# Strassen's seven products for the q, k and recurrence-gate blocks of the second projection

## The chip, the cores and the metric

The kernel runs on one core of a Trainium2 chip. The metric is the device time of one execution in microseconds (us); lower is better. Three runs of the kernel before gave 1884.34, 1887.08 and 1887.52 us, median 1887.08 us.

## The reference, cut to what matters

Two transformer-like blocks follow each other on 2048 tokens of width 1024, all in 32-bit floats. The change lies in the input projection of the second block, which turns the normalised tokens `h` (2048 x 1024) into 36 groups of 128 columns and 16 gate columns:

```python
proj = h @ w_in + b_in
(na_q, na_k, na_v, na_z, ml_q, ml_k, ml_v, ml_o, ml_z,
 i_f, f_f, i_b, f_b) = jnp.split(proj, split_idx, axis=-1)
na_out = neighbourhood_attention(na_q, na_k, na_v, rpb) * jax.nn.silu(na_z)
qk = jax.nn.silu(centred_short_conv(jnp.concatenate([ml_q, ml_k], axis=-1), conv_w, conv_b))
# ... chunkwise recurrence forward and backward over ml_q, ml_k, ml_v and the gates ...
ml_out = hm * jax.nn.silu(ml_z)
return jnp.concatenate([na_out, ml_out], axis=-1) @ w_out
```

`na_q`, `na_k` and `ml_z` (512 columns each) are the blocks that the change computes in another way. `na_q` and `na_k` feed the attention, which begins right after the projection; `ml_z` is read in the last stage.

## The kernel before, in words

A 32-bit product is made from three TensorE matmuls: each operand is split into a high part (a rounding copy on ScalarE, `split_high`) and a low part (a subtraction on VectorE, `split_low`), and `mm3` (L145, L146, L147) issues high x high, high x low and low x high into one PSUM bank.

**The projection** (class `Proj`). The 36 groups of 128 columns are called units, four to a block; before, the order of the blocks is nq, nk, mv, mk, mq, gates, nv, nz, mz, mo (`BLOCKS`). A piece of work `n` is one unit times 512 tokens (for mv, nv and mo: 128 tokens times a whole block); it is 8 k-tiles times three matmuls, so 24 matmuls with 512 columns. There are 144 of these and 4 short ones for the gates. All engines run over the same list `work`, and each does its share of `n` in program order. Six units of split weights lie in SBUF (`wa`, `wb`), and all four token blocks (`hT`) lie there split. Weights for a unit come through two raw buffers (`iraw`, 512 KB each, issued by SyncE at L1389). A result leaves PSUM through ScalarE or VectorE (for nq and nk both, as high and low part; for mo VectorE adds the bias at L1653 and ScalarE takes the sigmoid at L1578), and GpSimd issues its store to HBM (L1676, L1678, L1694, L1697).

**The states** (class `States`) are cut into 31 steps `s` that ride along with the projection: `states.pe(n)` and so on are called behind the projection's part of `n` on every engine, from `s0` on. A step is: SyncE loads keys `skC` (L2312; once turned, in the second half, `kTD` at L2318) and values `sv` (L2322); GpSimd weighs the values (L2378); TensorE multiplies (L2397, eight matmuls) and, in the first 16 steps, transposes the next keys (L2409); ScalarE copies and stores the transposed keys; VectorE updates `state` (L2358) once the store of the last one has landed; SyncE stores it (`CD`, L2327). Keys for transposition of step `s` may be loaded only when step `s-1` is transposed, since there is one buffer. In TensorE's program the product of step `s-1` and the transposes of step `s` stand behind work `n = s0 + s`. Before, `s0` lies 21 pieces of work behind the start of nv, and the states run during nz, mz and part of mo. `Gates` are 17 small steps that come first.

**The attention** takes over at the end of mo. Its first loads (`early_sp`: q and k heads `hd` at L1835, then z, v and the tables) are issued at works 3, 7 and 11 of mo; its first scores (`first_pe`) stand before the last piece of mo; its first mask table is made on GpSimd (L2017, L2024).

Of the kernel before, what the change touches and what calls it, by code (L numbers as in the profile page):

```python
# [5 lines left out]
F32 = mybir.dt.float32  # L6
# [4 lines left out]
P = 128  # L11
# [1193 lines left out]
BLOCKS = [("nq", 0), ("nk", 1), ("mv", 6), ("mk", 5), ("mq", 4), ("nv", 2), ("nz", 3), ("mz", 8), ("mo", 7)]  # L1205
# [3 lines left out]
class Proj:  # L1209


    NU = 6
# [3 lines left out]
    def __init__(self, k, banks, out, gw):  # L1216
# [24 lines left out]
        self.conv_u, self.conv_out, self.row_step, self.sign = k.sem("conv_u"), k.sem("conv_out"), k.sem("row_step"), k.sem("sign")  # L1241
# [3 lines left out]
        self.cols = [b * W + j * P for _, b in BLOCKS for j in range(4)]  # L1245
        work = []
        for bi, (name, b) in enumerate(BLOCKS):
            u0 = 4 * bi
            if name == "nv":
                work += [("gates", 0, tb) for tb in range(TB)]  # L1250
            if name in ROW_BLOCKS:
                work += [(name, u0, m) for m in range(NT)]
            elif bi == 0:
                work += [(BLOCKS[u // 4][0], u, tb) for tb in range(TB) for u in range(NU)]
            else:
                units = range(u0 + 2, u0 + 4) if bi == 1 else range(u0, u0 + 4)
                work += [(name, u, tb) for u in units for tb in range(TB)]
# [5 lines left out]
        for n, (name, u, tb) in enumerate(work):  # L1263
            first = len(jobs)
            if n == 0:
                jobs += [("w", 2), ("w", 3)]
            elif n < 3:
                jobs.append(("w", n + 3))
            if 2 <= n < 6:
                jobs.append(("h", 1, n - 2))  # L1270
            if n == 3 * NU:
                jobs.append(("gates",))
            if NU <= n < 3 * NU and u < 4:
                jobs.append(("h", tb + 1, u))
# [5 lines left out]
            while nu < min(more, 36):  # L1280
# [15 lines left out]
        self.stage, nst, self.convs = {}, 0, {}  # L1296
        for n, (name, u, tb) in enumerate(work):
            if name in ("mq", "mk"):
                self.convs[n] = len(self.convs)
            else:  # L1300
                self.stage[n] = nst
                nst += 2 if name in ("nq", "nk") else 1
        self.users = {}
        for n, i in self.stage.items():
            self.users[i] = n
            if work[n][0] in ("nq", "nk"):
                self.users[i + 1] = n

        self.evac_at, self.row_at, self.sign_at, c = {}, {}, {}, 0
        for n, (name, u, tb) in enumerate(work):  # L1310
            c += {"nq": 4, "nk": 1, "nz": 1, "mz": 1, "gates": 1, "mo": 1}.get(name, 0)
# [3 lines left out]
            if name in ("nq", "nk", "mz"):  # L1315
# [1796 lines left out]
```

## Time and profile before

| | |
|---|---|
| median of 3 runs | 1887.08 us |
| span of the profiled execution | 1883.3 us |
| TensorE matmul busy | 1865.6 us, 99% |
| VectorE, ScalarE, GpSimd busy | 982.4, 618.3, 552.5 us |
| mean HBM traffic | 161 GB/s |
| projection with states | from 598 to 1442 us |

The profiled execution has no other time of its own than its span from the first to the last instruction; the 3.8 us between it and the median are what lies around it and the spread of the runs. Matmuls are pipelined: the 0.39 us that the page gives for one is its stay in the array, and a new one starts every 0.23 us.

### The profile page before, as it was taken

Reading aid. Unit: us, or ns where it says so; the run is one execution under the profiler, and the core shown is the slowest. Engines: PE = TensorE matmul, PEld = TensorE weight load, DVE = VectorE, ACT = ScalarE, POOL = GpSimd, SP = SyncE. Lnnn points to the kernel's source line nnn. Section 1 sums busy time; section 2 is a strip of 40 time slices with the busy share of each in tenths; the row PEclk is TensorE's granted clock in tenths of the full one; section 3 lists DMA queues with packets and bytes.
Section 4 is the critical chain, followed back from the end, with each engine's and each line's share of the span. In section 5 each row is a group of like instructions: output and inputs, shape, how many; then the busy total and the mean of one; then the engine's idle time right before and its main releaser. Section 6 shows DMA issues by size and latency. Waiting matters only on the chain.

```text
span 1883.3 us, 26698 instructions
## 1 busy us (share of the span) xinstructions
PE 1865.6 (99%) x10035; PEld 1540.4 (82%) x10035; DVE 982.4 (52%) x2117; ACT 618.3 (33%) x1317; POOL 552.5 (29%) x925
## 2 busy tenths in 40 slices
PE   9999999999999999999999999999999999999998
PEld 8888878888888888888888787888887777788886
DVE  6556565775666433114777322223213777776665
ACT  7321111233444432101222202221114667655552
POOL 2112222233642222110110000222314777544442
PEclk9999999999999999999999999999999999999999
DMA  6223142366897745312221123665563776867663
GB/s 197 95 79 119 62 128 81 104 184 235 306 266 252 235 168 162 101 50 84 74 78 68 53 62 116 211 211 171 168 220 105 243 232 224 271 219 241 230 229 112
DMA packets 236365, 303.55 MB, mean 161 GB/s; under 512 B 41414, under 2 KB 161126, under 8 KB 236204
## 3 DMA queue, kind: packets, MB, share of 16 engines
q1 hardware_dynamic: 205724, 215.84, 37.4%
q0 software_dynamic: 23600, 77.61, 11.4%
q10 hardware_dynamic: 6912, 8.39, 1.2%
q8 instruction: 80, 1.31, 0.3%
q14 instruction: 49, 0.40, 0.1%
HBM read 194.71 MB, written 107.54 MB: 160 GB/s over the span
## 4 chain that ended last, share of the span: by engine, by line
PE 94%; DVE 2%; DMA 2%; issue 1%; ACT 1%; POOL 0%; SPq 0%; POOLq 0%; DVEq 0%; ACTq 0%
PE banks L145 25%; PE banks L147 25%; PE banks L146 25%; PE banks L2106 3%; PE banks L2069 3%; PE banks L2088 3%; PE banks L2704 2%; PE banks L2706 1%; PE banks L2397 1%; DMA iraw<-in_w_in 1%; PE banks L2089 1%; PE banks L2674 1%; PE banks L234 1%; PE banks L1109 1%; PE banks L1741 0%
## 5 line engine op out<-in xcount | busy, mean ns | idle before, releaser
L145 PE MATMUL banks<-hT,wu 128*128 128x512 f32 (+1 forms) x528 | 204.6, 387 | 1.1 <-DVE wu L512 0.6
L147 PE MATMUL banks<-hT,wu 128*128 128x512 f32 (+1 forms) x528 | 202.3, 383 | 0.0
L146 PE MATMUL banks<-hT,wu 128*128 128x512 f32 (+1 forms) x528 | 202.2, 383 | 0.0
L145 PE MATMUL banks<-iT,wub 128*128 128x512 f32 x384 | 151.2, 394 | 0.0
L145 PE MATMUL banks<-iT,wua 128*128 128x512 f32 x384 | 150.8, 393 | 0.0
L145 PE MATMUL banks<-wub,iT 128*128 128x512 f32 x384 | 150.6, 392 | 0.0
L147 PE MATMUL banks<-iT,wub 128*128 128x512 f32 x384 | 149.7, 390 | 0.0
L147 PE MATMUL banks<-iT,wua 128*128 128x512 f32 x384 | 149.5, 389 | 0.0
L146 PE MATMUL banks<-wub,iT 128*128 128x512 f32 x384 | 149.5, 389 | 0.0
L147 PE MATMUL banks<-wub,iT 128*128 128x512 f32 x384 | 149.5, 389 | 0.0
L146 PE MATMUL banks<-iT,wua 128*128 128x512 f32 x384 | 149.5, 389 | 0.0
L146 PE MATMUL banks<-iT,wub 128*128 128x512 f32 x384 | 149.4, 389 | 0.0
L1653 DVE TENSOR_TENSOR st<-banks,br 128x512 f32<-128x512 f32 x48 | 33.1, 692 | 201.0 <-PE banks L147 193.5
L145 PEld LDWEIGHTS banks<-hT,wu 128*128 128x128 f32 x528 | 99.3, 188 | 25.3 <-ACT ub L470 4.3
L147 PEld LDWEIGHTS banks<-hT,wu 128*128 128x128 f32 x528 | 99.2, 188 | 19.6
L146 PEld LDWEIGHTS banks<-hT,wu 128*128 128x128 f32 x528 | 99.3, 188 | 18.5
L1932 ACT ACTIVATE p<-s,ast 128x480 f32<-128x480 f32 (+1 forms) x128 | 83.7, 655 | 53.0 <-DVE ast L1970 53.0
L145 PE MATMUL banks<-ws,ys 128*128 128x512 f32 x256 | 100.5, 393 | 0.0
L147 PE MATMUL banks<-ws,ys 128*128 128x512 f32 x256 | 99.8, 390 | 0.0
L146 PE MATMUL banks<-ws,ys 128*128 128x512 f32 x256 | 99.7, 389 | 0.0
L1618 DVE SCALAR_TENSOR_TENSOR ca<-cu,cw,ca 128x512 f32<-128x512 f32 (+2 forms) x128 | 96.3, 752 | 4.5
L2039 POOL TENSOR_SCALAR p<-p,ast 128x384 f32<-128x384 f32 (+1 forms) x128 | 71.9, 562 | 46.2 <-DVE ast L1976 44.8
(293 smaller groups left out, 4116.3 us busy)
## 6 DMA issues: line engine op xcount, KB each, us to landing
iraw<-in_w_in SPq DMA_DIRECT2D x36, 512.0 KB, 4.4
wa<-in_w_ada SPq DMA_DIRECT2D x48, 256.0 KB
yT<-sg POOLq DMA_DIRECT2D x32, 256.0 KB, 3.1
oraw<-yT SPq DMA_DIRECT2D x32, 256.0 KB, 4.8
xr<-in_x SPq DMA_DIRECT2D x16, 512.0 KB, 4.4
h<-h POOLq DMA_DIRECT2D x16, 512.0 KB, 4.3
hT<-tr POOLq DMA_DIRECT2D x16, 512.0 KB, 5.1
tws<-wg SPq DMA_DIRECT2D x16, 512.0 KB, 5.1
```

The costliest lines, as they stand in the source:

```text
L145: e.matmul(ps, lh, rh, start=first, stop=False)
L146: e.matmul(ps, lh, rl, start=False, stop=False)
L147: return e.matmul(ps, ll, rh, start=False, stop=last)
L234: t = e.transpose(self.tp[m][g][:, j * P:(j + 1) * P], self.x[m][:, (4 * g + j) * P:(4 * g + j + 1) * P], self.ident[:])
L1618: e.scalar_tensor_tensor(out=a[:, left:right], in0=cur[:, left + x:right + x], scalar=cw[:, x, ch:ch + 1], in1=a[:, left:right], op0=ALU.m ...
L1653: e.tensor_tensor(self.st[i % 2][:], pb, self.br[:, x % 2, :], ALU.add).then_inc(*self.row_step.inc())
L1932: e.activation(self.pr[n % 8][:, 0:N], self.sr[n % 4][:, 0:N], ACT.Exp, bias=self.st[:, n, 0:1], scale=-1.0, accum_out=self.st[:, n, 1:2]) ...
L2039: e.tensor_scalar(rows[:, :, 0:P], rows[:, :, 0:P], self.st[:, n, 2:3], 1.0, ALU.mult, ALU.mult).then_inc(*self.scaled.inc())
L2069: t = e.matmul(self.pS[(2 * p + hh) % 4][:, 0:N], b[r, q, (2 * i + a) * P:(2 * i + a + 1) * P], keys, start=x == 0, stop=x == 2)
L2088: e.transpose(self.pT[x][:, j * P:(j + 1) * P], probs[:, 160 * j:160 * j + P], self.ident[:])
L2106: t = e.matmul(self.pO[d, 0:P], v, self.ptr[(2 * q + hh) % 4][r, j * P:(j + 1) * P], start=(j == 0), stop=(j == nb))
L2704: t = e.matmul(o, self.eb[c % 2][d][:, h, :], self.v1[c % 2][:, h, :], start=True, stop=not self.inter(c, d))
```

## The change

The nq, nk and mz units leave `Proj` and go into a new class `Fast`, which runs between the projection and the attention. `Proj` keeps 24 units in the order nz, mk, mv, mq0, mq1, nv, mq2, mq3, gates, mo (`PLAN`) and starts with 5 units instead of 6. The states' steps start at the second work of mo (`g0`), so that 31 steps of the recurrence lie, but for their gates part, in `Fast`: one step behind every second product.

`Fast` works on six "doubles": three pairs of unit pairs (nq0,1 with nk0,1; nq2,3 with nk2,3; mz0,1 with mz2,3) for each half of the tokens (1024). A pair of units times two token blocks of 512 is a 2 x 2 block product, and so are the two halves of the inner dimension; Strassen's rule makes it from 7 products with half the inner length in place of 8. A product is 4 k-tiles times three matmuls, 12 matmuls with 512 columns. There are 84 (`N`), 14 in a double, and 48 outputs. Sums of token quarters (128 x 2048) and of weight quarters (128 x 512) are made on GpSimd, their high parts on ScalarE, their low parts on VectorE. Token sums stay for the three doubles of a half; weight sums are made for each product, in 8 slots. Products that belong to several outputs are added in PSUM, and partial sums go through `part` on VectorE.

```diff
+    N, ND, OUTS, SLOTS = 84, 6, 48, 8
+    SEQ = [(i, q) for i, q in ((5, 0), (5, 1), (2, 0), (2, 1), (1, 0), (3, 0), (1, 1), (3, 1), (4, 0), (4, 1), (6, 0), (6, 1), (7, 0), (7, 1))]
...
+        self.early_x = {7: (0, 5), 9: (0, 2), 11: (0, 1), 13: (0, 3), 15: (0, 4)}
+        self.late_x = {1: (0, 6), 5: (0, 7), 30: (1, 5), 37: (1, 2), 38: (1, 3), 40: (1, 1), 42: (1, 4), 45: (1, 6), 47: (1, 7)}
...
+        self.early_t = {15: (0, 1)}
...
+        for n in range(1, self.ND):
+            for p in range(14):
+                self.late_t[14 * n - 3 + 8 * p // 13].append(14 * n + p)
...
+    def slot_free(self, w, j):
+        if j >= self.SLOTS:
+            w.wait_ge(*self.full.ge(j - self.SLOTS + 1))
...
+    def unit_load(self, e, dst, n, q, sem):
+        name, j0 = self.DOUBLES[self.ORDER[n][1]][q]
+        for u in range(2):
+            c = COLUMNS[name] * W + (j0 + u) * P
+            e.dma_start(dst[u][:], self.proj.win[:, :, c:c + P]).then_inc(*sem.inc())
...
+    def early_act(self, e, w, m):
+        if m in self.early_x:
+            self.tokens_high(e, w, *self.early_x[m])
+        for j in self.early_t.get(m, ()):
+            self.weights_high(e, w, j)
...
+    def sp(self, e, att):
...
+        for j in range(self.N):
+            n, p = divmod(j, 14)
+            if p == 6 and n + 1 < self.ND:
+                w.wait_ge(*self.t_lo.ge(14 * n + 14))
+                self.unit_load(e, self.rx, n + 1, 0, self.rx_in)
+                if n:
+                    self.unit_load(e, self.ry, n + 1, 1, self.ry_in)
+            if j == 8:
+                for x in range(2):
+                    self.quarter_load(e, self.kept[x], 1, (0, x), self.kept_in)
+            for i, at in ((2, 32), (1, 35), (4, 38), (6, 40), (7, 42)):
+                if j == at:
+                    self.tokens_load(e, w, 1, i)
+            att.early_sp(e, w, j)
+            if j % 2 == 0:
+                self.states.sp(e, w, self.nw + j // 2)
...
+    def dve(self, e, att):
...
+            if i == 5:
+                w.wait_ge(*self.full.ge(j + 1))
...
+                e.tensor_copy(part[:], self.pp[q]).then_inc(*self.copied.inc())
...
+            for x in self.late_t[j]:
+                self.weights_low(e, w, x)
+            if j in self.late_x:
+                self.tokens_low(e, w, *self.late_x[j])
+            if j % 2 == 0:
+                self.states.dve(e, w, self.nw + j // 2)
...
+    def pe(self, e, att):
...
+            elif i == 1:
...
+                    w.wait_ge(*self.w_out.ge(4 * n + (3 if q else 0)))
...
+            w.wait_ge(*self.t_lo.ge(j + 1))
...
+            for c in range(KT // 2):
+                e.matmul(ps, t[:, 0, c], x[:, 0, c], start=new and c == 0, stop=False, skip_group_check=not new)
+                e.matmul(ps, t[:, 0, c], x[:, 1, c], start=False, stop=False, skip_group_check=not new)
+                m = e.matmul(ps, t[:, 1, c], x[:, 0, c], start=False, stop=c == KT // 2 - 1, skip_group_check=not new)
+            m.then_inc(*self.full.inc())
+            if j % 2 == 0:
+                self.states.pe(e, w, self.nw + j // 2)
```

`early_sp`, `early_pool`, `early_act` and `early_dve` of `Fast` are called at the works `m` of mo. The attention's early loads move to products 74, 78 and 80, its mask table to product 82, its first scores stand before product 83. The program is emitted in three parts in place of two; all parts stand in one block, with no barrier between them.

## Rows read from the trace of the kernel before

**Rows 1.** The page's parts 1 and 4: busy time, and the chain that ended last.
```profile
PE 1865.6 (99%) x10035; PEld 1540.4 (82%) x10035; DVE 982.4 (52%) x2117; ACT 618.3 (33%) x1317; POOL 552.5 (29%) x925
...
PE 94%; DVE 2%; DMA 2%; issue 1%; ACT 1%; POOL 0%; SPq 0%; POOLq 0%; DVEq 0%; ACTq 0%
```

**Rows 2.** Who waited, TensorE: us in total, times, longest us.
```profile
PE banks L2240 <- DVE dg L2213: 1.8, 1, 1.8
...
PE banks L2069 <- DVE st L1653: 0.8, 1, 0.8
```

**Rows 3.** The chain in order of time: start, us, what; loads and a state's products.
```profile
1145.88 5.25 DMA iraw<-in_w_in
...
1153.51 4.35 DMA iraw<-in_w_in
...
1183.70 0.89 PE banks L2397 x8
1190.52 0.89 PE banks L2397 x8
...
1304.04 0.89 PE banks L2397 x8
1310.38 0.89 PE banks L2397 x8
```

**Rows 4.** Groups of instructions: out<-in, shape, count | busy us, mean ns | idle before.
```profile
L1653 DVE TENSOR_TENSOR st<-banks,br 128x512 f32<-128x512 f32 x48 | 33.1, 692 | 201.0 <-PE banks L147 193.5 <-DMA mo<-st 7.4
L2378 POOL TENSOR_TENSOR swv<-sv,wT 128x516 f32<-128x516 f32 x30 | 32.0, 1066 | 1.5 <-DMA sv<-mv 0.8
L2358 DVE SCALAR_TENSOR_TENSOR state<-state,dcB,banks 128x129 f32<-128x129 f32 x112 | 31.5, 343 | 47.5 <-DMA CD<-state 44.6 <-PE banks L2397 2.8
L1438 ACT ACTIVATE wub<-iraw 128x1024 fp32r<-128x1024 f32 x24 | 25.3, 1058 | 128.1 <-PE banks L147 85.5 <-DMA iraw<-in_w_in 42.7
L1188 DVE TENSOR_TENSOR glo<-graw,ghi 128x512 fp32r<-128x512 f32 x16 | 10.3, 683 | 0.0
L1578 ACT ACTIVATE st<-st 128x512 f32<-128x512 f32 x16 | 10.1, 632 | 78.2 <-DVE st L1653 78.2
L1694 POOL DMA_DIRECT2D mzc<-st x16 | 12.7, 793 | 75.2 <-DVE st L1639 75.2
```

**Rows 5.** One line's instructions, GpSimd and VectorE: duration ns min/median/max.
```profile
L1203 POOL TENSOR_TENSOR graw<-graw,grow x16: 1284/1447/2271, 446.1 to 532.8; 128x512 f32<-128x512 f32 x16
...
L1443 DVE TENSOR_TENSOR wub<-iraw,wub x24: 1215/1226/2812, 603.1 to 1299.4; 128x1024 fp32r<-128x1024 f32 x24
```

**Rows 6.** DMA issues, 1050 to 1440 us: count, KB each, median us to landing.
```profile
CD<-state SPq DMA_DIRECT2D x30, 258.0 KB, 3.5
sv<-mv SPq DMA_DIRECT2D x30, 256.0 KB, 3.4
...
skC<-mk SPq DMA_DIRECT2D x16, 256.0 KB, 3.2
...
vm<-VM SPq DMA_DIRECT2D x2, 512.0 KB, 6.1
z<-nz SPq DMA_DIRECT2D x2, 512.0 KB, 8.1
...
v<-VE SPq DMA_DIRECT2D x2, 32.0 KB, 7.5
```

**Rows 7.** SyncE's issues in order of time: start us, us, line, out<-in.
```profile
1397.51 0.80 SPq L1845 DMA_DIRECT2D vm<-VM  x2
1398.35 1.51 SPq L1840 DMA_DIRECT2D z<-nz  x2
1399.91 1.20 SPq L1862 DMA_DIRECT2D v<-VE  x2
```

**Rows 8.** Stretches: us, busy PE, PEld, DVE, ACT, POOL, PEclk, DMA share, GB/s.
```profile
1878.00:1883.30 5.30, 0.00 (x0) 0.00 (x0) 1.28 (x1) 0.00 (x0) 0.00 (x0) 0.51 0.25 99
```

**Rows 9.** ScalarE in order of time at the change to the attention.
```profile
1440.52 1.28 ACT L1578 ACT_TABLE_LOAD   x1
```

More of the change, by code:

```diff
@@ L1314, in __init__ @@
                 self.row_at[n] = len(self.row_at) + 1
[L1315 to L1316 removed]
         self.mo0 = next(n for n, x in enumerate(work) if x[0] == "mo")
[L1319 to L1321 removed]
+        self.g0 = g0 = next(n for n, x in enumerate(work) if x[0] == "gates")
+        self.place = [n % 8 if n < g0 else (g0 + (n - g0) % 5) % 8 for n in range(len(work))]
+        a, b, c = ((g0 + i) % 8 for i in (5, 6, 7))
+        self.reserved = [b, c, a]
     def pg(self, n):
@@ L1891, in sp @@
         proj, states = self.proj, self.states
-        w.wait_ge(*proj.full.ge(len(proj.work)))
+        w.wait_ge(*self.fast.full.ge(self.fast.N))
         for i in range(2):
             w.wait_ge(*proj.ca_st[i].ge(16))
-        for name in ("mv", "mz", "mo"):
+        for name in ("mv", "mo"):
             proj.stored_all(w, name)
-        w.wait_ge(*proj.row_step.ge(48))
+        self.fast.stored(w, self.fast.OUTS)
+        self.fast.read(w)
         states.stored_all(w)
@@ L2383, in pe @@
             for b in self.proj.reserved:
-                self.proj.read_out(w, max(x for x in range(self.proj.nv0) if self.proj.place[x] == b))
+                self.proj.read_out(w, max(x for x in range(self.proj.g0) if self.proj.place[x] == b))
         self.g.pe(e, w, n - self.g0)
@@ L2995, in whole @@
         mixer = Mixer(k, hT, banks, norm)
+        over = [x for x in k.used[first:] if x not in (mixer.full, mixer.y_step)]
         out = FirstOut(k, banks, mixer, ident, mhalf)
         gw = GatedWeights(k, out)
-        ended = k.used[first:]
+        ended = [x for x in k.used[first:] if x not in over]
         proj = Proj(k, banks, out, gw)
         states = States(k, proj, ident)
-        att = Attention(k, proj, states, ident)
         with k.nc.Block() as block:
@@ L3025, in pool @@
                 out.pool(e, gw)
-                proj.pool(e, att, states)
             def pe(e):
@@ L3032, in pe, with sp1, act1, dve1 @@
                 out.pe(e)
-                proj.pe(e, att, states)
             k.emit(block, sp, act, dve, pool, pe)
+            k.retire(over)
+            fast = Fast(k, proj, states)
+            att = Attention(k, proj, fast, states, ident)
+            def sp1(e):
+                proj.sp(e, fast, states)
+                fast.sp(e, att)
+            def act1(e):
+                proj.act(e, fast, states)
+                fast.act(e, att)
+            def dve1(e):
+                proj.dve(e, fast, states)
+                fast.dve(e, att)
+            def pool1(e):
+                proj.pool(e, fast, states)
+                fast.pool(e, att)
+            def pe1(e):
+                proj.pe(e, states)
+                fast.pe(e, att)
+            k.emit(block, sp1, act1, dve1, pool1, pe1)
             k.retire(ended)
```

534 lines of the change are left out of this document (406 added, 128 removed).

## Prediction

> **What bounds the kernel now.** I read the page's busy line first: TensorE's matmuls fill 99% of the span, and the chain that ended last lies on TensorE for 94% of it [rows 1]. Then the list of who waited: the longest wait on TensorE in the projection is 1.8 us, for a gate step on VectorE, and 0.8 us more falls at the change to the attention [rows 2]. So TensorE's issue rate is the bound; fewer matmuls are worth their full time, and every wait that the change adds costs its full time too. Last the chain in order of time, for the price of one matmul: one piece of work and one state step take 1310.38 - 1304.04 = 6.34 us, of which 0.89 us are the step's eight products [rows 3]. That leaves 5.45 us for 24 matmuls, 0.227 us each. In the first half of the states the period is 1190.52 - 1183.70 = 6.82 us [rows 3], so the transposes cost another 0.48 us.
>
> **What it removes.** 48 pieces of 24 matmuls (1152) become 84 products of 12 (1008): 144 x 0.227 = 32.7 us. The 1.8 us wait of the gate step [rows 2] goes too: VectorE now makes its operand two works earlier, with no weights to wait for. Together 34.5 us. Starting with five units instead of six, and nz in place of nq, takes work from VectorE; TensorE was not waiting there, so I cost it at nothing. The states' steps keep their number and place one behind 24 matmuls' time, as before.
>
> **What it adds, by the order of each engine's program.** A product lasts 12 x 0.227 = 2.73 us. I write T for the end of product 14n+5, the sixth of double n.
>
> (a) The way into `Fast`. The weights of product 0 are split at work 15 of mo, behind the evacuation of that same work. After the last matmul of mo come VectorE's addition 0.69, ScalarE's sigmoid 0.63 [rows 4], the high part of token quarter (0,4), its low part, and the weights' low part 0.68 [rows 4]. A high part of 1024 elements takes 1.06 us and 512 take 0.63 [rows 4], so 2048 take 1.06 + 2 x 0.43 = 1.9; a low part of 1024 takes 1.23 [rows 5] and 512 take 0.68 [rows 4], so 2048 take 2.3. Sum 6.2, with four hand-overs 6.4 us, all of it idle TensorE. Nothing covers it.
>
> (b) Double 0. GpSimd can start the token sum (0,6) at 10.4 us (behind the weight sum whose slot product 0 frees at 9.1). At 1.28 to 2.27 us for 512 elements [rows 5] a sum of 2048 takes 5.1 to 9.1. Then 1.9 on ScalarE, 2.3 on VectorE, and in VectorE's order six operations of 0.69 up to the subtraction that product 6 waits for: 24 to 28 us, where TensorE comes to it at 6.4 + 6 x 2.73 = 22.8. Cost 1 to 5, taken 2.
>
> (c) **SyncE's queue**, the largest item. At product 14n+6 SyncE waits for the last weights of the double, and only then issues four loads of 512 KB (two in double 0); the keys and values of the state step stand behind them in its program. The last weights' slot comes free at T; GpSimd's sum 1.3 [rows 5], ScalarE 0.63, VectorE 0.68 [rows 4] make it T + 2.9. Queued behind the wait is the load of `skC`, and TensorE wants it at T + 2.73 + 0.89 = T + 3.6, behind product 14n+6. Before, the load went out as soon as the last transposes were done, and landed 3.2 us later [rows 6], under a whole piece of work. Least cost: four issues of 0.4 [rows 7], its own 0.4, landing 3.2: T + 8.1, a stall of 4.5. Most cost: the loads are served one behind the other. For that speaks that a load of only 32 KB took 7.5 us to land [rows 6] when 2 MB had been issued in the 2.4 us before it [rows 7], so about 10 us for the lot; two loads of 512 KB landed within 5.7 us [rows 3]. Then `skC` lands at T + 2.9 + 10 + 1 = T + 13.9, a stall of 10.3. The 32 KB row is nearest to this case, so I take 9 us each at products 20 and 34. In double 0 only 1 MB stands ahead and no product of a state stands before the transposes: 4.6 to 6.9, taken 6.3. At product 8 two quarters of 1 MB go ahead of the next keys: 0 to 3, taken 2. At product 32 SyncE waits for the end of product 31 and issues two quarters of 1 MB ahead of the keys: 0.8 to 7, taken 6. At products 48 and 62 the transposes are over; there the values come late: T + 9.9 to T + 16 with 1.07 on GpSimd [rows 4], wanted at T + 3 x 2.73 + 0.89 = T + 9.1, and the last state's store, which VectorE waits for, stands behind them too. 0.8 to 7, taken 6 each. Sum 6.3 + 2 + 9 + 6 + 9 + 6 + 6 = 44.3 us; the low ends make 16.0, the high ends 51.5.
>
> The Trainium skill says the same of the queue in another way (DMA: Bandwidth & Descriptors, "Queues, rings and completion order"): descriptors of one ring are consumed in order. By that rule the item would be near 51.5 us, by separate service near 16.0; the 32 KB row agrees with the rule.
>
> (d) The token sums of the second half. From product 36 to 48 TensorE needs 12 x 2.73 + 6 x 0.89 = 38.1 us. GpSimd has three token sums (15.4), eight weight sums (10.4), seven stores of mz at 0.79 and five state weights at 1.07 [rows 4, 5], 36.7 us, about 4 us of lag at the start, and some 3 us of waits for values behind 1 MB loads; the splits of quarter (1,6) and the subtraction add 4.9. TensorE's product 48 waits for that subtraction: 48.6 - 38.1 = 10. If GpSimd's operations overlap its waits better it is 3, with sums at 2.27 over 20. Taken 7.
>
> (e) The way out. ScalarE must take the silu of the last gate block, with a table load of 1.28 us [rows 9] between the first exponentials and the next, and VectorE waits for it before it goes on with the attention. 0 to 4 us, taken 2. The attention's loads, issued over the last 10 products (27 us; before it was 12 works), land about when they are wanted.
>
> (f) The clock. The stretch at the very end, with no matmul in it, shows a granted clock of 0.51 [rows 8], and four of the stalls above (at 0, 20, 34 and 48) are longer than its 5.3 us. If the engine comes back at 1.2 GHz, the lower of its two levels, a product costs up to 2.73 us more: 0 to 2.7 for each of four, taken 1.4, sum 5.6.
>
> Sum: 6.4 + 2 + 44.3 + 7 + 2 + 5.6 = 67.3 us added, 34.5 removed, net +32.8. Against the profiled execution's span: 1883.3 + 32.8 = 1916.1 us. The median of the runs before lies 3.8 above the span, so 1920 us.
>
> **Rivals.** One: the order of the programs costs what I say, but the big loads don't hold up the small ones. Then (c) is 16.0 and, with shorter stalls, (f) is 0: 6.4 + 2 + 16.0 + 7 + 2 = 33.4 added, so -1.1 and 1886 us. Against it speaks the 32 KB row [rows 6, 7]; for it, that the states' loads kept a median of 3.2 to 3.4 us [rows 6] with other traffic beside them. Two, the other side: the waits that I see on SyncE's queue and GpSimd are hidden, because TensorE's program reaches the state steps later than I count or keys come earlier, and only (a), (b) and (e) stay: 1887 - 34.5 + 10.4 = 1863 us. The point from which it decides is that the stalls sum to less than 34.5 us; it needs (c) under 17. Three: GpSimd is over capacity, its sums at the slow end of 2.27 us because VectorE's subtractions run beside them. Then (b) is 5, (d) 20, and the last weights come 1 us later in five doubles: some 21 us more, 1941 us. Four: the clock. If every stall of over 6 us, eight of them, brings the lower level back, (f) is 8 x 2.7 = 22 instead of 5.6, and the time 1936 us. The Trainium skill has this as a rule (TensorE: Matmul & The Clock Gate, "Why this matters for your kernels"): idle gaps between bursts of matmuls put the array back to the low clock. Five: the change doesn't do what it says, since more matmuls are issued than 12 for a product; the code shows three in each of four rounds, so nearly excluded.
>
> **How the numbers follow.** The forecast has 0.52, rival one 0.18, two 0.14, three and four together 0.15, five 0.01. The range reaches from 1874 (half of the way between rivals one and two) to 1944. A difference under 0.2% (3.8 us) is about what a measurement of this kernel can't tell from none. Faster by more than that: rival two and a third of rival one, 0.21; same: 0.07; slower: 0.72.
>
> **What the trace after would show.** Some 1008 matmuls in `Fast` at 0.227 us apart; idle TensorE of 6 us at the end of mo with a VectorE low part as releaser; at the transposes behind products 6, 20 and 34 idle time of 6 to 10 us released by the DMA of `skC`, right behind four loads of weights on SyncE; behind product 50 and 64 a wait for the weighed values or for `state`; at product 48 a wait for VectorE's subtraction. If `skC` lands 3 to 4 us after its issue though four loads stand ahead, rival one holds. If TensorE's idle time in the whole stage is under 15 us, the reading of SyncE's order is wrong.

## The result, and the profile after

| | before | after |
|---|---|---|
| median, 4 runs each | 1885.7 us | 2026.9 us |
| ratio | | 1.0757 (1.074 to 1.0775) |
| span of the profiled execution | 1883.3 us | 2031.6 us |
| end of the projection with states | 1442 us | 1577 us |

The change makes the kernel 7.6% slower. The forecast was slower, but by 33 us; it is 141. The profiled execution of the changed kernel is the longest of its four (the spans of the others are 2024.3 to 2025.8 us), so what is added up from its trace comes to some 6 us more than the medians give. The page's parts 1 and 4, which answer to [rows 1]:

```profile
PE 1880.4 (93%) x9891; PEld 1543.7 (76%) x9891; DVE 1161.4 (57%) x2231; ACT 677.0 (33%) x1365; POOL 678.6 (33%) x995
...
PE 76%; DVE 8%; DMA 5%; issue 5%; POOL 2%; ACT 2%; SPq 2%; POOLq 0%; DVEq 0%; ACTq 0%
```

TensorE has 144 matmuls fewer (10035 to 9891), as the code says, and is busy 15 us longer all the same. The chain, 94% TensorE before, now runs through VectorE, DMAs and issues for a fifth. Who waited, TensorE (us in total, times, longest), which answers to [rows 2]:

```profile
PE banks L2803 <- DVE state L2764: 43.3, 9, 9.1
PE banks L2815 <- DMA skC<-mk: 39.4, 4, 12.3
PE banks L2159 <- issue: 17.4, 2, 10.0
PE banks L2159 <- DVE fpart L2081: 14.0, 2, 8.4
PE banks L2646 <- DVE mpB L2624: 4.8, 1, 4.8
PE banks L2494 <- POOL e L2446: 3.9, 1, 3.9
PE banks L2803 <- DVE state L2761: 3.2, 1, 3.2
```

From the last matmul of mo (ends at 1150.5 us) to the last product (1577.4) are 426.9 us. At the price of [rows 3], 84 x 2.73 + 30 x 0.89 + 16 x 0.48 + 1.6 for two gate steps and the attention's first scores (an estimate) is 265.3. Of the 161.6 us between, 122.2 are idle (19 waits of over 0.3 us); the other 39 I put down to matmuls at a low clock. Stretches, in the columns of [rows 8]: three of 5 us right behind stalls, the whole stage, and the start of the attention:

```profile
1271.40:1276.40 5.00, 4.95 (x14) 4.08 (x15) 1.13 (x4) 0.60 (x1) 1.05 (x1) 0.50 0.43 136
1333.30:1338.30 5.00, 4.98 (x14) 4.12 (x15) 1.12 (x4) 1.88 (x2) 1.05 (x1) 0.50 0.26 96
1551.60:1556.60 5.00, 4.96 (x12) 3.95 (x13) 1.58 (x3) 0.00 (x0) 0.78 (x1) 0.50 0.98 339
1584.00:1600.00 16.00, 13.35 (x65) 8.52 (x66) 5.94 (x20) 5.35 (x15) 9.12 (x21) 0.50 0.61 158
1153.80:1580.00 426.20, 305.95 (x1338) 251.58 (x1340) 263.26 (x348) 111.89 (x176) 195.66 (x183) 0.84 0.57 179
```

The granted clock (seventh value) is 0.50 in all but the row of the whole stage, the lower of the two levels: behind the stalls 12 to 14 matmuls start in 5 us, where 22 do at 0.227 us.

Two things in the trace explain most of the idle time. The first was forecast: SyncE's queue. Its issues in order of time (columns of [rows 7]):

```profile
1259.24 1.09 SPq L1938 DMA_DIRECT2D frx<-in_w_in  x2
1260.38 4.37 SPq L1938 DMA_DIRECT2D fry<-in_w_in  x2
1264.79 2.18 SPq L2718 DMA_DIRECT2D skC<-mk  x1
1267.02 0.87 SPq L2728 DMA_DIRECT2D sv<-mv  x1
1267.93 0.82 SPq L2733 DMA_DIRECT2D CD<-state  x1
```

Four loads of 512 KB, then the keys, and TensorE goes on at 1271.45, 12.2 us behind the first of these issues. The second was not forecast. VectorE, then GpSimd, in the same stretch (start us, us, line, what):

```profile
1537.67 0.68 DVE L2073 COPY fpart<-banks 128x512 f32<-128x512 f32 x1
1538.28 7.90 DVE L1871 TENSOR_TENSOR ft<-fts,ft 128x512 fp32r<-128x512 f32 x2
1546.10 0.68 DVE L2073 COPY fpart<-banks 128x512 f32<-128x512 f32 x1
```

```profile
1539.40 1.30 POOL L1852 TENSOR_TENSOR fts<-fry 128x512 f32<-128x512 f32 x1
1540.65 1.29 POOL L1852 TENSOR_TENSOR fts<-frx,frx 128x512 f32<-128x512 f32 x1
1541.89 1.29 POOL L1852 TENSOR_TENSOR fts<-fry,fry 128x512 f32<-128x512 f32 x1
1543.14 1.26 POOL L1852 TENSOR_TENSOR fts<-frx,frx 128x512 f32<-128x512 f32 x1
1544.37 1.25 POOL L1852 TENSOR_TENSOR fts<-fry,fry 128x512 f32<-128x512 f32 x1
```

The 7.90 us are two low parts of 0.69 us each when nothing holds them. The first takes that; the second starts at 1538.87, half a microsecond ahead of the first of GpSimd's five sums, and lasts 7.30 us, until 0.55 us behind the end of the last one. GpSimd is not slowed here: 1.25 to 1.30 us a sum, as alone. That VectorE is held off by GpSimd, and not late for another reason, had to be shown by experiment.

### The profile page after: what moved, and what is told of

The parts are those of the page before. It is cut to its first block, busy times and chain, and to the rows that moved or that the text cites. A ratio compares the mean times of both kernels' runs of the same rounds, so it can differ in the third digit from the quotient of the medians.

```text
span 2031.6 us, 26803 instructions
## 1 busy us (share of the span) xinstructions
PE 1880.4 (93%) x9891; PEld 1543.7 (76%) x9891; DVE 1161.4 (57%) x2231; ACT 677.0 (33%) x1365; POOL 678.6 (33%) x995
## 4 chain that ended last, share of the span: by engine, by line
PE 76%; DVE 8%; DMA 5%; issue 5%; POOL 2%; ACT 2%; SPq 2%; POOLq 0%; DVEq 0%; ACTq 0%
PE banks L145 19%; PE banks L147 18%; PE banks L146 18%; PE banks L2512 3%; DVE ft L1871 3%; PE banks L2475 2%; PE banks L2494 2%; DMA CD<-state 2%; PE banks L2159 2%; PE banks L2160 1%; PE banks L2161 1%; DMA skC<-mk 1%; PE banks L3110 1%; PE banks L3112 1%; SPq L1938 1%
## 5 line engine op out<-in xcount | busy, mean ns | idle before, releaser
L2159 PE MATMUL banks<-fx,ft 128*128 128x512 f32 x336 | 147.2, 438 | 31.4 <-issue 17.4
L2160 PE MATMUL banks<-fx,ft 128*128 128x512 f32 x336 | 141.6, 421 | 0.0
L2161 PE MATMUL banks<-fx,ft 128*128 128x512 f32 x336 | 140.6, 418 | 0.0
L2159 PEld LDWEIGHTS banks<-fx,ft 128*128 128x128 f32 x336 | 70.9, 211 | 47.5 <-issue 18.4
L145 PE MATMUL banks<-iT,wua 128*128 128x512 f32 x256 | 99.8, 390 | 0.0
L147 PE MATMUL banks<-iT,wua 128*128 128x512 f32 x256 | 99.6, 389 | 0.0
L146 PE MATMUL banks<-iT,wua 128*128 128x512 f32 x256 | 99.6, 389 | 0.0
```

The costliest lines, as they stand in the source:

```text
L145: e.matmul(ps, lh, rh, start=first, stop=False)
L146: e.matmul(ps, lh, rl, start=False, stop=False)
L147: return e.matmul(ps, ll, rh, start=False, stop=last)
L2159: e.matmul(ps, t[:, 0, c], x[:, 0, c], start=new and c == 0, stop=False, skip_group_check=not new)
L2160: e.matmul(ps, t[:, 0, c], x[:, 1, c], start=False, stop=False, skip_group_check=not new)
L2161: m = e.matmul(ps, t[:, 1, c], x[:, 0, c], start=False, stop=c == KT // 2 - 1, skip_group_check=not new)
```

## The experiments

My theory after the result: most of the missing 108 us is VectorE held off while GpSimd's sums run (and what comes late through it), with SyncE's queue at about its forecast size. The rivals: the queue is worth far more than its term, or the low clock is. "After" below is 2026.9 us; the kernel before took 1884 to 1886 us beside every group of runs.

**The queue.** First, only the order: the recurrence's loads and store of the step go ahead of the wait and the four loads.

```diff
-            if p == 6 and n + 1 < self.ND:
-                w.wait_ge(*self.t_lo.ge(14 * n + 14))
-                self.unit_load(e, self.rx, n + 1, 0, self.rx_in)
-                if n:
-                    self.unit_load(e, self.ry, n + 1, 1, self.ry_in)
...
             if j % 2 == 0:
                 self.states.sp(e, w, self.nw + j // 2)
+            if p == 6 and n + 1 < self.ND:
+                w.wait_ge(*self.t_lo.ge(14 * n + 14))
+                self.unit_load(e, self.rx, n + 1, 0, self.rx_in)
+                if n:
+                    self.unit_load(e, self.ry, n + 1, 1, self.ry_in)
```

> SyncE's part at product 14n+6 is turned round: the state step's loads and store first, then the wait for the last weights and the four unit loads. Queue theory: the waits for the keys at products 6, 20 and 34 (12.3, 11.4 and 10.2 us in the trace of the changed kernel) and those for the state's store after 48 and 62 (9.1 and 8.1 us) go, each with some 2.5 us at the low clock behind it: about 1965 us from 2027. The wait of 5.4 us at product 32 stays. Port theory (GpSimd's sums hold VectorE off, and VectorE is what comes last anyway): VectorE's waits take over, no more than 15 us are won, 2012 to 2027 us.

Measured: 2016.6 us (ratio 1.0691, 1.0656 to 1.0727). A miss: the waits for keys only moved one step on.

```profile
PE banks L2815 <- DMA skC<-mk: 34.8, 4, 13.8
PE banks L2803 <- DVE state L2764: 34.2, 10, 8.9
```

The 2 MB take longer to land than the 6.3 us of a step, so whichever keys come next stand behind them. The second try keeps the wait ahead and puts only the loads behind the keys:

> Only the order of the loads is turned round; the wait for the last weights of the double stays ahead of the state's loads. If the loads ahead in the queue are what costs, the keys land 3.5 us after their issue and the stalls at 6, 20 and 34 shrink from 10 to 12 us to about 3 to 4 us: about 1985 us. If the wait itself is what costs, they shrink by less than half: 2005 us or more.

Measured: 2023.0 us (1.0725, 1.0694 to 1.0756), keys 36.1 us in seven waits. A miss too: the stalls behind 20 and 34 shrank to 2.4 and 2.2 us, but 6.1 and 8.0 us came up behind 22 and 36. So neither the wait in SyncE's program nor the order within one step is most of the cost; the bulk of the loads is. Then the loads one at a time, over products 6 to 9, and the kept token quarters at 12 and 14, always behind the step's own loads:

```diff
...
+            if n + 1 < self.ND and 6 <= p < 10:
+                w.wait_ge(*self.t_lo.ge(14 * n + 14))
+                u, q = (1, 1, 0, 0)[p - 6], p % 2
+                if n or not q:
+                    name, j0 = self.DOUBLES[self.ORDER[n + 1][1]][q]
+                    c = COLUMNS[name] * W + (j0 + u) * P
+                    e.dma_start((self.ry if q else self.rx)[u][:], self.proj.win[:, :, c:c + P]).then_inc(*(self.ry_in if q else self.rx_in).inc())
+            if j in (12, 14):
+                self.quarter_load(e, self.kept[(j - 12) // 2], 1, (0, (j - 12) // 2), self.kept_in)
```

> The four unit loads of 512 KB are issued one at a time at products 6, 7, 8 and 9 of a double, the kept token quarters at products 12 and 14, and every load stands behind the state step's loads and store. Queue theory: no load of the keys has more than 1 MB ahead of it, so it lands within 5 us and the stalls for the keys (39 us in four) fall under 10 us in all; the waits of 9 and 8 us for the state's store in doubles 3 and 4 go: 1960 to 1975 us. Port theory alone: VectorE is late anyway and takes the gain: 2005 us or more.

Measured: 1995.9 us (1.0579, 1.0544 to 1.0614), 31 us gained where 52 to 67 were expected, and the waits for keys fall from 39.4 to 13.6 us:

```profile
PE banks L2804 <- DVE state L2765: 33.2, 9, 8.9
...
PE banks L2816 <- DMA skC<-mk: 13.6, 5, 4.1
```

The state waits stay. VectorE waited 61.0 us for the state's store in the changed kernel, so that store alone went to ScalarE's queue, issued at the odd products:

```diff
-        s -= 2
+    def keep(self, e, w, n):
+        k, s = self.k, n - self.s0 - 1
         if 0 <= s < self.STEPS and s != NT - 1:
             c, d, i = self.at(s)
...
             if j % 2 == 0:
                 self.states.act(e, w, self.nw + j // 2)
+            else:
+                self.states.keep(e, w, self.nw + j // 2)
```

> Nothing left out: the changed kernel with one edit, the store of the recurrence's state issued from ScalarE's queue one product after its update and no longer behind the loads in SyncE's. VectorE waited 61.0 us in eleven waits for that store, and TensorE 43.3 us for VectorE's state. Theory, that most of it is the store's place in SyncE's order (a wait for the low parts or for products in front of it): VectorE's wait falls under 35 us, TensorE's under 25 us, and with what other waits take over 2012 us (2004 to 2019). Rival, that it is the store's transfer behind 2 MB of loads, which another queue doesn't change: the longest waits stay near 10 us, 2020 to 2027 us.

Measured: 2030.4 us (1.0765, 1.0749 to 1.0781), no gain. VectorE's waits in this run:

```profile
DVE fso L2053 <- ACT fso L2022: 42.1, 7, 15.9
DVE fso L2049 <- ACT fso L2020: 31.2, 6, 14.6
...
DVE state L2768 <- DMA CD<-state: 7.4, 4, 2.7
```

The theory's two waits come out as said (VectorE's for the store 61.0 to 7.4, TensorE's for the state 43.3 to 24.9), but not its time. ScalarE, which now waits to issue the store, is late with the outputs (VectorE's waits for them were 22.7 and 9.3 us in the changed kernel, 42.1 and 31.2 here), and TensorE waits 18.1 us for weighed values in the place of the state. The wait changed its place.

**The sums.** First the 60 weight sums from GpSimd to VectorE, each ahead of its low part.

> The ten sums of weights of a double (128x512) move from GpSimd to VectorE, right ahead of the low parts of the same step; the token sums stay on GpSimd. Port theory: VectorE pays 10 x 0.69 = 6.9 us for a double and no longer stands up to 7 us behind a row of GpSimd sums: 20 to 40 us faster, 1985 to 2005 us. If VectorE's own load is the bound, 10 to 40 us slower.

Measured: 2012.5 us (1.067, 1.0639 to 1.0701), 14 us gained, less than the 20 to 40 expected. The gate step's wait of 4.8 us is gone and the stall of 8.45 us at product 76 is 2.24, but keys and state waits stay. Then all sums cut to one element, so that their order and hand-overs stay and their work goes (the sums are left out: this kernel doesn't compute them). The cut for the tokens; the one for the weights is alike:

```diff
-        e.tensor_tensor(xa, first, second, op).then_inc(*self.x_sum.inc())
+        e.tensor_tensor(xa[:, 0, 0:1], first[:, 0, 0:1], second[:, 0, 0:1], op).then_inc(*self.x_sum.inc())
```

> GpSimd's sums of weights and tokens are cut to one element for a partition, and the splits read the first operand instead; this kernel leaves the sums out, and its products are of other numbers. Port theory (while GpSimd works through sums one behind the other, VectorE's operations on two SBUF operands do not start): VectorE's low parts of 128x512 never take more than 0.75 us (7.3 us before), TensorE's waits for partial sums (5.5 and 8.5 us) go, those for the state fall by half, the first stall falls from 10.0 to 6.4 us: 1960 to 1980 us from 2027. Queue theory alone: the keys' stalls of 10 us and more stay and at most 15 us are won, 2012 us or more.

Measured: 1956.8 us (1.0372, 1.034 to 1.0404), 70 us gained. That is the largest single term. Between the two profiled stages lie 58 us of idle time (122.2 and 64.6) and 18 us of slow matmuls. But it takes two things away at once, the adds that may hold VectorE off and the time that high and low parts wait for a sum. So the adds were given back where nobody waits for them (the sums are left out here too):

```diff
+    def idle_sums(self, e, w, n):
+        for _ in range(n):
+            self.sums += 1
+            same = self.scratch[self.sums % 2][:]
+            ...
+            w.wait_ge(*self.scr.ge(self.sums - 2))
+            e.tensor_tensor(same, same, same, ALU.add).then_inc(*self.scr.inc())
```

> The kernel without sums (1956.8 us) again, so the sums of the weights and tokens stay left out, but GpSimd is given the same amount of adding at the same places into a scratch buffer that nobody reads and nobody waits for: three adds of 128x172 in the place of each 128x512 sum, twelve in the place of each token sum. Theory of the shared way to the buffers (GpSimd's back-to-back adds hold off VectorE's operations on two buffers): most of the 70 us come back although no wait depends on an add, 2005 to 2027 us, and the longest weight low part (L1871) goes from 1.5 us back to 5 to 8 us. Rival, the chain (what cost 70 us was that the high and low parts wait for the sum itself): the adds are read by nobody, so the time stays at 1957 within 5 us, and the longest low part stays near 1.5 us.

Measured: 1995.7 us (1.0583, 1.0561 to 1.0605). That lies between the two expectations: 39 of the 70 us come back from adds whose results nobody waits for. The low parts, by operand (duration ns min/median/max), in the changed kernel, without sums, and with the adds into scratch:

```profile
L1871 DVE TENSOR_TENSOR ft<-fts,ft x60: 673/693/7298, 1172.5 to 1552.5; 128x512 fp32r<-128x512 f32 x60
```

```profile
L1871 DVE TENSOR_TENSOR ft<-fry,ft x35: 672/684/1547, 1200.9 to 1471.5; 128x512 fp32r<-128x512 f32 x35
```

```profile
L1883 DVE TENSOR_TENSOR ft<-fry,ft x35: 674/927/11824, 1209.6 to 1511.6; 128x512 fp32r<-128x512 f32 x35
```

The one of 11.82 us starts at 1292.80; GpSimd has adds, a state weight and adds again, without a gap, from 1291.30 until past 1302.75:

```profile
1292.80 11.82 DVE L1883 TENSOR_TENSOR ft<-fry,ft 128x512 fp32r<-128x512 f32 x1
```

```profile
1293.58 5.20 POOL L1864 TENSOR_TENSOR fscratch<-fscratch 128x172 f32<-128x172 f32 x12
1298.75 1.04 POOL L2797 TENSOR_TENSOR swv<-sv,wT 128x516 f32<-128x516 f32 x1
```

So it is shown that adds alone hold VectorE off. That this costs all of the 39 us is not shown: whatever stands behind the adds in GpSimd's program (the one-element sums, the weighed values, the stores) is late by them as well, and this run doesn't divide the two. The other 31 us are not explained by it; that high and low parts wait for a sum is the candidate, and the runs don't divide them further. Last, the reason why one low part stands for a whole train: GpSimd was made to wait for each sum's end before its next instruction.

```diff
         e.tensor_tensor(self.ts[j % self.SLOTS][:], self.quarter(j, a), self.quarter(j, b), op).then_inc(*self.t_sum.inc())
+        w.wait_ge(*self.t_sum.ge(self.t_sums[j]))
```

> Nothing left out: the changed kernel, where GpSimd waits behind each sum of weights or tokens for that sum's own end before it starts its next instruction. Nobody needs these waits; they only open a gap between two sums, where they ran back to back (five sums in 6.2 us while a low part of 0.69 us on VectorE stood for 7.3 us). Theory of turns: VectorE is held off as long as GpSimd's instructions follow one another without a gap and gets in at the first gap. Then a 0.69 us low part takes at most one sum's time more, 2.0 us (behind a token sum 5.7 us), and a good part of the adds' 39 us comes back: 1995 to 2015 us, from 2026.9. Rival, that the gap is too short to matter or GpSimd's next sum wins it again: longest low parts stay over 5 us, time within 4 us of 2027 or above it by the gaps' own cost.

Measured: 2003.6 us (1.0625, 1.0607 to 1.0642), 23 us gained by waits that nobody needs. GpSimd has the same sums to do here and only more waits, so the gain must come from the other side, VectorE, and trains without a gap cost at least 23 us. As far as the runs show, the price of the hold-off lies between these 23 us and e8's 39; of my theory's "most of the missing 108 us" that leaves about a third at best. The low parts now:

```profile
L1872 DVE TENSOR_TENSOR ft<-fts,ft x60: 674/1057/5090, 1167.0 to 1523.1; 128x512 fp32r<-128x512 f32 x60
L1872 DVE TENSOR_TENSOR ft<-frx,ft x12: 693/1016/2428, 1153.1 to 1500.6; 128x512 fp32r<-128x512 f32 x12
```

They are slower in the middle (0.69 to 1.06 us) and faster at worst: VectorE gets in at the first gap. What is left of 5.09 us lies behind a token sum, one instruction of 5.0 us.

**The way in.** The stall at the end of mo, with the first two weights split one work earlier.

```diff
-        self.early_t = {15: (0, 1)}
+        self.early_t = {14: (0, 1)}
```

> The weights of products 0 and 1 are split at work 14 of mo and no longer at work 15. Both theories: the stall of 10.0 us at the way into the new part goes or falls under 2 us, and with it the low clock of the next 4 us (2 us): 2014 to 2017 us from 2027. If product 0 waits for anything else, the stall stays at 5 us or more.

Measured: 2023.6 us (1.0726, 1.0659 to 1.0793), no difference (two runs, 9 us apart, and neither reaches the 2014 to 2017 expected). The stall moved from product 0 to product 2, whose weights stand behind token quarter (0,4) on VectorE, and grew:

```profile
1167.40 0.77 PE L2159 MATMUL banks<-fx,ft 128*128 128x512 f32 x1 [11.90 <-issue]
```

**Together.** Early split, loads one at a time and weight sums on VectorE:

> The early split of products 0 and 1, the spread loads and the ten weight sums on VectorE together. If the three causes add: 12 + 50 + 20 us, about 1945 us, with a mean granted clock of 0.98 or more. If they only hide one another (each alone gives 10 to 15 us because the next wait takes over), this gives more than the sum of the three alone.

Measured: 1974.0 us (1.0463, 1.0428 to 1.0499). The three alone gained 3.3 + 31.1 + 14.5 = 48.9 us, together 52.9, so they add; 1945 us was expected because each alone had been hoped to be worth more. Then three repairs on the kernel without sums: loads one at a time, products 2 and 3 split ahead of quarter (0,4), which goes behind product 3, and the state's store on ScalarE (sums left out).

```diff
-        self.early_t = {15: (0, 1)}
+        self.early_t = {14: (0, 1), 15: (2, 3)}
-        self.early_x = {..., 13: (0, 3), 15: (0, 4)}
+        self.early_x = {..., 13: (0, 3)}
-        self.late_x = {1: (0, 6), 5: (0, 7), ...}
+        self.late_x = {1: (0, 6), 3: (0, 4), 5: (0, 7), ...}
```

> The kernel without sums (1956.8 us; sums left out) with three repairs on top: the loads one at a time behind the recurrence's (alone -31 us), the split of products 2 and 3 ahead of the token split of product 8 at the way in, and the store of the state moved from SyncE's queue to ScalarE's, one product earlier. Theory: what is left in the kernel without sums is loads (34.7 us in four waits for the keys), the state (22.7 us, most of it a store that waits its turn behind the same loads) and the way in (6 to 13 us), with some 5 to 10 us of slow clock behind them; all of it goes but a third: 1900 us (1888 to 1915), near the kernel before. Rival, that the state waits come from the engines and not from the queue: state waits stay over 20 us and the time is over 1915.

Measured: 1910.6 us (1.0133, 1.0116 to 1.015): the repairs are worth 46 us. TensorE's waits from 1145 us on:

```profile
PE banks L2820 <- DMA skC<-mk: 9.8, 4, 3.1
PE banks L2478 <- DVE fso L2036: 8.5, 1, 8.5
PE banks L2808 <- POOL swv L2789: 6.0, 2, 3.4
PE banks L2808 <- DVE state L2769: 5.2, 5, 2.3
```

The last product ends at 1448.2 us, 6 us behind the projection's end of before; the other 19 us of the difference fall at the change to the attention. The same repairs with the sums where they were:

> Nothing left out: the changed kernel, its sums on GpSimd as they were, with the three repairs of e9 (loads one at a time, products 2 and 3 split ahead, the state's store on ScalarE's queue). If the causes add up, the repairs are worth the 46 us that they were worth without sums (1956.8 to 1910.6): 1981 us (1973 to 1990), which leaves 70 us between this kernel and e9 for the sums. Rival, that they cover one another (a product that waits for its low part also covers its keys): the repairs are worth under 35 us here, over 1992 us. Against e10 (the same with the sums on VectorE, 1973.5 us) it tells what the engine of the sums is worth: by the adds into scratch (39 us) GpSimd's should be the dearer by 10 us or more.

Measured: 1983.8 us (1.0526, 1.0509 to 1.0544): 43 us for the repairs here, 46 without sums, so the causes add up. With the 60 weight sums and the seven later token sums on VectorE (three token sums, made during mo, stay on GpSimd):

> Nothing left out: all sums on VectorE (weights and the second half's tokens; the early token sums too), loads one at a time, products 2 and 3 split ahead of product 8's tokens, the state's store on ScalarE's queue. From the combination of 1974.0 us: way in -8, state -15, token sums -3: 1948 us (1935 to 1960), so still slower than the kernel before (1886). Rival, that VectorE is then the bound in the second half (its added work is 50 sums at 0.7 us and 10 at 2.3 us, 58 us in 430): no gain over 1974, with waits for the low parts (L1871, L1932) in the place of the removed ones.

Measured: 1973.5 us (1.0468, 1.0453 to 1.0484). Against e11 the engine of the sums is worth 10 us, as said; the 1948 hoped for is a miss, and the rival's "no gain over 1974" holds, though TensorE waits for VectorE's partial sums (21.1 us in five waits) and not, as the rival said, for low parts. With GpSimd's sums one at a time instead:

> Nothing left out: the same waits in the kernel with the three repairs and GpSimd's sums (1983.8 us; with the sums on VectorE 1973.5). Theory of turns: 1960 to 1976 us. Rival: 1980 us or more.

Measured: 1975.6 us (1.0485, 1.0469 to 1.05), as good as VectorE's sums within the intervals. Against e11 the waits of GpSimd are worth 8 us, where they were worth 23 in the changed kernel: e11's stalls of 9.1 us at product 2 and 2.7 at product 6 have become one of 16.1 at product 6. No version with its sums comes near the kernel before; even the one without them is 1.3% slower.

**The clock.** TensorE transposes the identity in the four long waits for keys, in front of the wait, so that nothing waits for other things than it did.

```diff
+            for h in range({0: 40, 7: 36, 13: 12, 14: 32}.get(s, 0)):
+                e.transpose(self.pT[:, 0:P], self.ident[:], self.ident[:])
             w.wait_ge(*self.k_in.ge(s + 1))
```

> Nothing left out: the changed kernel with TensorE kept busy in the four long waits for the recurrence's keys (12.3, 11.4, 5.4 and 10.2 us, behind products 6, 20, 32 and 34): 40, 36, 12 and 32 transposes of the identity into the bank that the keys' transposes fill next, ahead of the wait for the keys; nobody reads them. At 0.1 to 0.2 us each they fill 4 to 8 us of the longest waits and end before the keys land. Theory, that the slow clock behind a stall costs time of its own (the granted clock was 0.50 in the 5 us after 1271.4 and after 1333.3 us): the clock behind these four is 0.9 or more and the time falls by 5 to 10 us, to 2017 to 2022 us. Rival, that the products behind a stall wait for something else soon after anyway: the clock rises, the next waits take the gain, 2024 us or more. Second rival, that transposes of the identity don't raise the clock: clock and time stay (2027 us).

Measured: 2027.3 us (1.0751, 1.0733 to 1.0769). It tells little: the transposes took 0.113 us each, 7.8, 7.5, 4.9 and 7.0 us of the waits stayed idle behind them, and the clock in 5 us behind the waits was 0.89, 0.97, 0.68 and 0.63. With 104, 96, 44 and 86:

> As e13_kept_busy, with 104, 96, 44 and 86 transposes of the identity (0.113 us each there: 11.8, 10.8, 5.0 and 9.7 us) so that TensorE works until the keys land; in e13 it still stood still for 7.8, 7.5, 4.9 and 7.0 us before them and the clock behind was at 0.63 to 0.89. Theory, that the slow clock behind these four stalls costs time of its own: the four stalls are under 2 us each, the clock in the 5 us behind them is 0.95 or more, and the time falls by 4 to 8 us, to 2019 to 2023 us. Rival, that what runs behind a stall has to wait again soon: clock up, time within 2 us of 2027. Second rival, that identity transposes don't hold the clock: clock 0.5 to 0.7 behind them and the time stays.

Measured: 2023.4 us (1.0731, 1.0713 to 1.0749). Behind the same waits the clock is now whole:

```profile
1202.00:1207.00 5.00, 5.00 (x27) 4.13 (x25) 0.75 (x1) 1.50 (x3) 1.15 (x3) 1.00 1.07 377
1271.00:1276.00 5.00, 5.00 (x26) 4.21 (x26) 1.76 (x5) 1.11 (x3) 1.38 (x3) 1.00 0.67 210
1333.00:1338.00 5.00, 5.00 (x30) 4.37 (x29) 2.48 (x4) 1.99 (x3) 1.52 (x2) 1.00 0.11 40
1353.00:1358.00 5.00, 5.00 (x30) 4.34 (x29) 2.77 (x2) 1.28 (x2) 3.94 (x2) 1.00 0.39 134
```

In the changed kernel these stretches have 0.61, 0.50, 0.50 and 0.70, which is 5 x (0.39 + 0.50 + 0.50 + 0.30) = 8.5 us of slow time. The kernel gains 3.5 us of it by the medians, and waits for the state rise from 46.5 to 49.7 us. The stage alone, in the two profiled executions, is 5.9 us shorter. All four runs lie below all four of the changed kernel, but the intervals of the two ratios overlap, so the size is rough. By these two figures 40 to 70% of the slow time is a cost of its own; the rest would have been a wait anyway.

## Why the prediction was wrong

**Right.** 144 matmuls fewer at 0.227 us; TensorE as the bound whose every wait counts in full; the places: the stall at the end of mo, at products 6, 20, 32, 34 by the keys, at 48 by VectorE's subtraction, at 50 and 64 by the state. Their forecast sum at these places was 55.7 us, and they measure 72.1.

**(a)** The way in: 6.4 forecast, 10.04 measured. In the kernel without sums it is 6.22, so the step's reckoning was right and the rest is VectorE held off: the low part of quarter (0,4) took 6.10 us at 1153.87 beside four weight sums, where it takes 2.28 alone.

**(b)** Double 0: 2 forecast at product 6, none measured, because the way in and a gate step had made TensorE late already: in e4, e8, e11 and e16, where TensorE comes to it earlier, product 6 waits 2.7 to 16.1 us for VectorE. But the gate steps wait: 1.5, 1.5 and 1.2 us still in mo and 4.8 in double 0, where I had struck out the one wait of 1.8 in [rows 2] as gone. All four are gone in the kernel without sums.

**(c)** SyncE's queue: 44.3 forecast. Product by product (forecast, measured): 6: 6.3, 12.3; 20: 9, 11.4; 32: 6, 5.4; 34: 9, 10.2; 50: 6, 9.1; 64: 6, 8.1; product 8: 2, none. One at a time, the loads are worth 31 us, and with state and way in 46. The mechanism held and the size was low: 12.2 us from the first load's issue to the keys' use, where I had 11 (T + 2.9 to T + 13.9). The six stalls sum to 56.6 us, above my high end; in the kernel without sums they are 8.6, 11.2, 5.5, 9.4, 8.8 and 7.5, sum 51.0. That is near the 51.5 which, by my estimate, the Trainium skill's order of one ring (DMA: Bandwidth & Descriptors, "Queues, rings and completion order") gives. Rival one, that loads don't hold up small ones, falls with e1 and e6; rival two with it.

**(d)** Token sums of the second half: 7 forecast, 5.5 measured at product 48. What I left out is every other product whose sums run beside VectorE: among others stalls of 7.39 us at 1383.97 (product 42) and 8.45 at 1551.63 (product 76), and waits for the state of 8.90 at 1318.18 and 4.47 at 1243.95. Ten waits at products where I had forecast none sum to 45.3 us; in the kernel without sums the waits at such places sum to 7.0.

**The step that failed** is how [rows 5] were read. The GpSimd row with its maximum of 2271 ns and the VectorE row with its 2812 ns beside a median of 1226 were both there, and rival three took the first alone, as GpSimd made slower by VectorE. The trace of the kernel before shows each row's cause, one in each direction:

```profile
446.12 2.39 DVE L1009 SCALAR_TENSOR_TENSOR h<-hr,ost,fw 128x1024 f32<-128x1024 f32 x1
447.39 2.27 POOL L1203 TENSOR_TENSOR graw<-graw,grow 128x512 f32<-128x512 f32 x1
```

```profile
1273.98 2.81 DVE L1443 TENSOR_TENSOR wub<-iraw,wub 128x1024 fp32r<-128x1024 f32 x1 [0.46 <-ACT wub L1438]
1274.63 1.07 POOL L2378 TENSOR_TENSOR swv<-sv,wT 128x516 f32<-128x516 f32 x1
```

The sum of 2.27 us ends 1.2 us behind VectorE's operation, the low part of 2.81 us 1.1 us behind GpSimd's. In the changed kernel the second kind prevails: in `Fast` VectorE's operations together take 88 us more than at their shortest (8 without sums), and GpSimd's 12. I took the low parts as 0.68 us everywhere, so no term of the sum had the cost in it: of the 70 us that sums cost, at least 23 are shown to be this and up to 39 may be, and of the 45.3 us of waits in (d) 38 go when the sums go. Rival three named the pair of engines and reached 1941 us by the lesser direction.

**(e)** The way out: 2 forecast. The waits are 1.25 + 3.87 + 2.22 = 7.3 us, and the attention starts at a clock of 0.50 for 16 us, where before it was 1.00; from the projection's end to the span's end are 454.2 us, before 441.0: 13 us. In e9 it is 460.3. I priced ScalarE's silu and its table alone. The rows show three waits one behind the other instead, for VectorE's last outputs (8.5 us in e9), for GpSimd's first probabilities (3.9, 3.7 in e9) and for VectorE's copy (2.2). Before, a piece of mo of 5.45 us stood behind the first scores, where now one product of 2.73 does, and TensorE waited 0.8 us [rows 2]; that this is the reason was not tested.

**(f)** The clock: 5.6 forecast, 39 us of slow matmul time in the stage, 18 of them gone without sums. Rival four said the mechanism (the Trainium skill, TensorE: Matmul & The Clock Gate, "Why this matters for your kernels", has it that idle gaps drop the clock; the trace agrees, with 0.50 in the stretches behind the stalls that end at 1271, 1333 and 1551 us). But by e14 only 3.5 to 5.9 of 8.5 us are a cost of its own; by that share 16 to 27 of the 39, an estimate from one pair of kernels. Rival four's 22 us lie in that range, and of the 108 missing the clock is then 10 to 22.

**The sum, made again from the runs.** 2026.9 - 1956.8 = 70 for the sums; 1956.8 - 1910.6 = 46 for loads, state and way in (50.7 stood in (a) and (c)); 1910.6 - 1885.9 = 25 left, which is 19 at the way out and 6 in the stage, where short waits (27.8 us) and a low clock (some 11) more than eat up the 34.5 us saved. The forecast's 33 were 67 added less 34.5; the runs have 176 added less 34.5. By the trace alone the added time is 72 us at the forecast places, 45 in the other waits of (d), 9 in the gate steps, 13 at the way out and 39 at a low clock.

What stays open: how much of e8's 39 us is the hold-off itself, and the 31 us of the sums that adds into scratch don't bring back. These are no question of the engine alone, since with VectorE's sums (e10) 63 us lie above e9 as well.

## What to carry to other kernels

Before work goes to GpSimd because it is idle, look at what VectorE does in the same microseconds: a maximum far above the median of a short operation on two buffers is the sign of it, and it multiplies with trains of GpSimd instructions; a gap behind each of them gave back 23 us here, and 8 in the repaired kernel. Bulk loads go one at a time between the small ones that a short loop waits for; reordering them within one step only moves the stall. A scheme that takes 2% of an engine's work away has no room for a new chain: count the waits it adds at each step first.

## What the runs showed of the hardware that I had not expected

GpSimd's two-operand adds hold off VectorE's operations that read SBUF alone: the low parts with their two buffers, and one that reads a single buffer (L2047, 4.05 us at 1361.41 in place of 0.49, beside a token sum of 4.61). VectorE's copies out of PSUM (676 to 692 ns in twelve) and its adds of PSUM and SBUF (671 to 690) keep their time beside them, while a low part of 0.69 us took up to 7.3, and 11.82 in e8. GpSimd loses little in the changed kernel: most sums keep 1.25 to 1.31 us, ten of 60 take more, and the longest, 3.31 us at 1420.69, stood behind a VectorE low part of 2.87. Where GpSimd's operations are short it is held as well: an add of 128x172, 0.46 us in the median of e8, took up to 2.52. The Trainium skill (SBUF — State Buffer, "SBUF: two separate sides") has a lock on a shared pair of ports, for which the one that starts first blocks the other for "the whole instruction". The pair of operations agrees with the trace, the length does not: by whole instructions the low part of 7.30 us would have waited for one sum of 1.3 us at most, and it waited for five, though by the trace it had started ahead of the first. What decides who goes next is not shown.

SyncE's issue of a DMA is itself slow behind bulk loads: the keys' load takes 0.36 us to issue when nothing stands ahead and 2.18 us behind the four loads, and two of these loads took 4.37.
